# The same block products for key and gate tiles, with the last two products of a pair exchanged and its bank sums in another order

## The reference

```python
def mlstm_project(h, w_in, b_in):
    p = h @ w_in + b_in
    q, k, v, o, gates = jnp.split(p, [hk, 2 * hk, 2 * hk + hv, 2 * hk + 2 * hv], axis=-1)
    ...
```

## Time and profile before

| | us |
|---|---|
| median of 3 runs | 2078.43 |
| lowest and highest run | 2077.24, 2079.9 |
| profiled execution, from its first to its last instruction (span) | 2076.5 |
| TensorE busy in it | 2014.3 |
| VectorE, ScalarE, GpSimd busy in it | 1223.6, 819.1, 989.1 |

### The profile page before, as it was taken

How to read it: one execution, slowest core, us unless ns; L and a number is a source line. 1 busy time by engine, 2 the same in 40 slices (tenths; PEclk the granted TensorE clock), 3 DMA queues, 4 the chain that set the end, 5 groups by cost and what they waited for, 6 DMA issues and landing times.

```text
span 2076.5 us, 24039 instructions
## 1 busy us (share of the span) xinstructions
PE 2014.3 (97%) x9167; PEld 1663.5 (80%) x9167; DVE 1223.6 (59%) x1276; ACT 819.1 (39%) x1066; POOL 989.1 (48%) x560
## 2 busy tenths in 40 slices
PE   6999999999999999999999999988999999999999
PEld 5788888888788888878887888766788888878877
DVE  6889998877642475545502565589655555523125
ACT  5343355566452323221123464445344334412135
POOL 1376655555222222123311446648877877722244
PEclk7999999999999999999999999999999999999999
DMA  9641122122112323448855865341222222253123
GB/s 377 216 142 41 54 63 63 56 68 74 41 61 81 121 83 101 146 115 283 278 161 160 279 230 163 93 151 61 62 61 61 80 83 87 66 193 125 46 89 127
DMA packets 269263, 251.42 MB, mean 121 GB/s; under 512 B 8330, under 2 KB 230291, under 8 KB 269155
## 3 DMA queue, kind: packets, MB, share of 16 engines
q1 hardware_dynamic: 266067, 238.42, 36.3%
q10 hardware_dynamic: 3088, 11.54, 1.4%
HBM read 206.08 MB, written 43.84 MB: 120 GB/s over the span
## 4 chain that ended last, share of the span: by engine, by line
PE 51%; issue 14%; POOL 6%; DVE 1%; DMA 1%; ACT 0%; POOLq 0%; SPq 0%; DVEq 0%; ACTq 0%
PE PS L2227 16%; PE PS L1739 16%; PE PS L2005 5%; PE PS L2119 5%; POOL wl L851 3%; PE PS L2241 1%; PE PS L2063 1%; PE PS L2064 1%; PE PS L2072 1%; POOL SCR L1042 1%; PE PS L1928 1%; PE PS L2052 1%; PE PS L2153 1%; POOL wl L1029 1%; POOL XL L1025 0%
## 5 line engine op out<-in xcount | busy, mean ns | idle before, releaser
L851 POOL TENSOR_TENSOR wl<-raw,wh 128x1024 fp32r<-128x1024 f32 (+1 forms) x157 | 377.6, 2406 | 807.9 <-ACT wh L1098 589.7
L1739 PE MATMUL PS<-XH,wh 128*128 128x512 f32 x1424 | 442.4, 392 | 7.2 <-POOL wl L851 3.0
L1739 PE MATMUL PS<-XH,wl 128*128 128x512 f32 x1424 | 441.1, 391 | 0.0
L1739 PE MATMUL PS<-XL,wh 128*128 128x512 f32 x1424 | 440.6, 391 | 0.0
L1739 PEld LDWEIGHTS PS<-XH,wh 128*128 128x128 f32 x1424 | 264.9, 188 | 64.0 <-POOL wl L851 4.0
L1739 PEld LDWEIGHTS PS<-XL,wh 128*128 128x128 f32 x1424 | 265.7, 188 | 54.1
L1739 PEld LDWEIGHTS PS<-XH,wl 128*128 128x128 f32 x1424 | 265.4, 188 | 53.5
L1098 ACT ACTIVATE wh<-raw 128x1024 fp32r<-128x1024 f32 (+1 forms) x108 | 111.0, 1028 | 436.9 <-PE PS L1739 187.2
L2470 DVE SCALAR_TENSOR_TENSOR PS<-B,PJ,PS 128x1022 f32<-128x1022 f32 (+7 forms) x197 | 251.1, 1275 | 7.5
L1171 ACT ACTIVATE wh<-raw 128x1024 fp32r<-128x1024 f32 x48 | 50.8, 1058 | 248.2 <-PE PS L1739 228.7
L1029 POOL TENSOR_TENSOR wl<-SCR,wh 128x512 fp32r<-128x512 f32 x80 | 114.2, 1429 | 69.7 <-ACT wh L1567 69.1
(11 more groups left out here) (439 smaller groups left out, 3747.8 us busy)
## 6 DMA issues: line engine op xcount, KB each, us to landing
B<-in_ada_w SPq DMA_DIRECT2D x48, 512.0 KB, 5.4
raw<-in_ffn_up_w SPq DMA_DIRECT2D x48, 512.0 KB, 4.1
raw<-in_w_in SPq DMA_DIRECT2D x40, 512.0 KB, 4.5
raw<-in_m_in_w SPq DMA_DIRECT2D x37, 512.0 KB, 5.0
mod_tiles<-in_mod_w SPq DMA_DIRECT2D x16, 512.0 KB, 13.2
raw<-in_w_out SPq DMA_DIRECT2D x16, 512.0 KB, 5.0
qkvo_d<-B SPq DMA_DIRECT2D x16, 512.0 KB, 3.5
raw<-in_m_out_w SPq DMA_DIRECT2D x16, 512.0 KB, 4.2
```

The lines of the kernel that those rows point to most:

```text
L851: tt(wl[slot][:, 0:kc, :], raw[slot][:, 0:kc, :], wh[slot][:, 0:kc, :].bitcast(F32), ALU.subtract).then_inc(lo_done, 1)
L1739: last = mm(ps[:, c:c + step_n], W[:, k, :], Y[:, k, c:c + step_n], start=(seen == 0), stop=(seen == total - 1))
```

## The change

The four key tiles and the eight tiles of o are no longer projected one by one. They become six pairs (O_PAIRS; the first two, K_PAIRS, are keys) of seven block products each, all of them after the value passes. In a pair, the products come in the order O_ORDER, the last two exchanged against the up projection, and VectorE adds the banks in the order O_SUMS. For this:

- The tokens need sums and differences too. VectorE makes twelve tiles of 128x512 (token_sum, two or three operations each), ScalarE their high halves (token_high) and GpSimd their low halves (token_low), all during the value passes. A fourth set (t3_sum: twelve operations on GpSimd) replaces the second half of XH and XL in blocks 0 to 3 when the value passes are over; its low halves (t3_low) stand on VectorE's list between the first bank sums of pair 0.
- The reversing copies stand behind the first evacuation of values. SyncE waits for the ten row stores before it loads the ninth value unit, and ScalarE and VectorE wait for them too.
- Of the 32 late tiles four are multiplied during the value passes and 28 behind the 28 bank sums of pairs 0 to 3, one each. TensorE waits for all 32 before pair 4, transposes the gate rows there, and runs the 32 columns inside pair 4.
- Biases, sigmoid, scale and the store of a pair's tiles are ScalarE's (o_finish), the store issued from its own queue.
- Two value units are loaded ahead of the wait for the gate rows' chain (lf_sb).

```diff
--- before.py
+++ after.py
...
+        def o_bank(q):
+            b = (q + (2 if q >= 7 * (O_PAIRS - 2) else 0)) % 8
+            return part(PS[b // 2], b % 2)
+
+        O_ORDER = (0, 1, 2, 3, 4, 6, 5)
+        O_SUMS = (1, 4, 3, 6, 3, 2, 5)
+
+        def o_place(q):
+            s, n = divmod(q, 7)
+            return s, O_ORDER[n]
...
+            for u in range(4, V_UNITS):
+                proj_unit(V_FIRST + u)
+                if u in (6, 10, 14):
+                    v_store((u - 6) // 4)
+                if u == 7:
                     rows_store()
-                if t == O_UNIT + 1:
                     sp.wait_ge(*at("rows_out", 16 * 10))
+                if u == V_UNITS - 1:
+                    for n in range(4):
+                        late_load(n)
...
+            def pair_load(s):
+                for v in range(2):
+                    if s == 0:
+                        sp.wait_ge(lo_done, PAIR_UNIT + 1 + v)
+                    else:
+                        sp.wait_ge(*at("oq_lo", 7 * s - 5 + v))
+                        sp.wait_ge(*at("os_ok", 4 * s))
+                    if s < O_PAIRS:
+                        sp.dma_start(raw[(PAIR_UNIT + v) % 2][:], cols_of(m_in_w, 0, KD, o_column(s) + P * v)).then_inc(ev(f"oq_in{v}"), 16)
+                    else:
+                        half_unit(v)
...
+            pair_load(0)
+            v_store(3)
+            for s in range(O_PAIRS):
+                pair_load(s + 1)
+                if s == 1:
                     for n in range(3):
                         sp.wait_ge(*at(f"v_out{n}", 16 * len(range(n, NCH * 2, 3))))
                     sp.dma_start(ROWS, rows_d[0:NCOL, :]).then_inc(ev("gate_rows_in"), 16)
+                if s < O_PAIRS - 2:
+                    for n in range(4 + 7 * s, 4 + 7 * (s + 1)):
+                        late_load(n)
+                elif s == O_PAIRS - 2:
+                    sp.wait_ge(*at("late_summed", LATE * KD))
                     for d in range(2):
                         chunk_load(0, d, 0, False)
...
+            sp.wait_ge(*at("late_ps", 1))
+            chunk_load(1, 0, 1, False)
+            sp.wait_ge(*at("oq_used", 7 * (O_PAIRS - 1) + 4))
+            chunk_load(1, 1, 1, False)
...
+            def t3_sum(n):
+                k, i = divmod(n, 3)
+                if i == 0:
+                    tt(t3_t[k], XH[:, k + HK, HALF:SEQ].bitcast(F32), XH[:, k, HALF:SEQ].bitcast(F32), ALU.subtract).then_inc(ev("t3_sum"), 1)
+                elif i == 1:
+                    if k:
+                        pool.wait_ge(*at("t3_sum", n - 1))
+                    tt(US[:], XL[:, k + HK, HALF:SEQ].bitcast(F32), XL[:, k, HALF:SEQ].bitcast(F32), ALU.subtract).then_inc(ev("t3_sum"), 1)
+                else:
+                    pool.wait_ge(*at("t3_sum", n))
+                    tt(t3_t[k], t3_t[k], US[:], ALU.add).then_inc(ev("t3_sum"), 1)
+
...
+            T3_AT = {0: (0, 2), 1: (2, 4), 2: (4, 6), 3: (6, 8), 4: (8, 9), 14: (9, 12)}
+            LOW_AT = {7: (0, 2), 9: (2, 4), 10: (4, 6), 11: (6, 8), 12: (8, 10), 13: (10, 12)}
+            for u in range(1 - Q_TILES, V_UNITS):
+                low(GxG.U + V_FIRST + u, (GxG.U + V_FIRST + u) % 2)
+                if u == 0:
+                    pool.wait_ge(*at("xl_Gx", KD))
+                elif u == 14:
+                    pool.wait_ge(*at("rows_out", 16 * 10))
+                for n in range(*T3_AT.get(u, (0, 0))):
+                    t3_sum(n)
+                for m in range(*LOW_AT.get(u, (0, 0))):
+                    token_low(m)
+
...
+            for q in range(7 * O_PAIRS):
+                o_low(q)
+                s, i = divmod(q, 7)
+                if 1 <= q <= 4:
+                    o_weight_sum(0, q - 1)
+                elif 6 <= q <= 9:
+                    o_weight_sum(1, q - 6)
+                elif i in (5, 6) and 0 < s < O_PAIRS - 1:
+                    for n in range(2 * i - 10, 2 * i - 8):
+                        o_weight_sum(s + 1, n)
+            low(G5.U, G5.U % 2)
...
+            HIGH_AT = {7: (0, 2), 9: (2, 6), 10: (6, 9), 11: (9, 12)}
+            for u in range(1, V_UNITS):
+                high_at(GxG.U + V_FIRST + u, 0)
+                if u == 7:
+                    act.wait_ge(*at("rows_out", 16 * 10))
+                for m in range(*HIGH_AT.get(u, (0, 0))):
+                    token_high(m)
+
+            def o_high(q):
+                s, i = o_place(q)
+                if i < 3:
+                    act.wait_ge(*at(f"oq_in{i // 2}", 16 * (s + 1)))
+                else:
+                    act.wait_ge(*at("os_ok", 4 * s + i - 2))
+                if q < 4:
+                    act.wait_ge(unit_used, PAIR_UNIT + 1 + q // 2)
+                else:
+                    act.wait_ge(*at("oq_used", q - 3))
+                f(ring(wh, q), o_weights(i), ACT.Copy).then_inc(ev("oq_hi"), 1)
+
+            def o_copy(s):
+                act.wait_ge(*at("oq_used", 7 * s + 1))
+                if s:
+                    act.wait_ge(*at("osum_ok", SUMS * s))
+                f(US[:], o_bank(7 * s), ACT.Copy).then_inc(ev("opair_copy"), 1)
...
+            for q in range(4):
+                o_high(q)
+            for k in range(HK):
+                act.wait_ge(*at("t3_sum", 3 * k + 3))
+                f(XH[:, k, HALF:SEQ], t3_t[k], ACT.Copy).then_inc(ev("t3_hi"), 1)
+            for s in range(O_PAIRS):
+                o_high(7 * s + 4)
+                o_copy(s)
+                if s:
+                    o_finish(s - 1, 0)
+                o_high(7 * s + 5)
+                o_high(7 * s + 6)
+                if s < O_PAIRS - 1:
+                    for i in range(4):
+                        o_high(7 * (s + 1) + i)
+                    o_finish(s, 1)
...
+            o_finish(O_PAIRS - 1, 1)
+            o_finish(O_PAIRS - 1, 0)
...
+            def o_product(s, i):
+                q = 7 * s + O_ORDER.index(i)
+                (W_H, W_L), (X_H, X_L) = (ring(wh, q), ring(wl, q)), o_tokens(i)
+                bank = o_bank(q)
+                pe.wait_ge(*at("oq_lo", q + 1))
+                earlier = [p for p in range(q) if o_bank(p) == bank]
+                if not earlier:
+                    pe.wait_ge(*at("v_sb", q + 13))
+                else:
+                    before, j = o_place(earlier[-1])
+                    if j == 0:
+                        pe.wait_ge(*at("opair_copy", before + 1))
+                    else:
+                        pe.wait_ge(*at("osum_ok", SUMS * (before + 1) - O_SUMS[::-1].index(j)))
+                if q == 7 * (O_PAIRS - 1):
+                    pe.wait_ge(*at("late_used", 1))
+                if s == 0 and i == 2:
+                    pe.wait_ge(*at("tk_lo", 3 * HK))
+                elif s == 0 and i == 6:
+                    pe.wait_ge(*at("t3_lo", HK))
+                for k in range(HK):
+                    for n, (W, Y) in enumerate(((W_H, X_H), (W_L, X_H), (W_H, X_L))):
+                        ins = mm(bank, W[:, k, :], Y[:, k, :], start=(k == 0 and n == 0), stop=(k == HK - 1 and n == 2))
+                        c = 12 * (i - 1) + 3 * k + n
+                        if s == O_PAIRS - 2 and 0 <= c < LATE * KD:
+                            late_column(c)
+                ins.then_inc(ev("oq_used"), 1)
+
+            for s in range(O_PAIRS):
+                if s == O_PAIRS - 2:
+                    pe.wait_ge(*at("gate_rows_in", 16))
+                    pe.wait_ge(*at("opair_copy", s))
+                    pe.wait_ge(*at("late_summed", LATE * KD))
+                    for c in range(NCH):
+                        last = nc.tensor.transpose(COLS_BANK[:, NCOL * c:NCOL * (c + 1)], ROWS[:, P * c:P * (c + 1)], ident[0:NCOL, 0:NCOL])
+                    last.then_inc(ev("cols_ps"), 1)
+                for i in O_ORDER:
+                    o_product(s, i)
...
+            def token_sum(m):
+                i, k, full = block_sum(m)
+                if m >= 4:
+                    dve.wait_ge(*at("tk_lo", m - 3))
+                x12, x11, x22, x21 = ((XH[:, c, h:h + HALF].bitcast(F32), XL[:, c, h:h + HALF].bitcast(F32))
+                                      for c, h in ((k, HALF), (k, 0), (k + HK, HALF), (k + HK, 0)))
+                if i == 0:
+                    step.link(V.tensor_tensor(full, x12[0], x11[0], ALU.subtract))
+                    step.link(V.tensor_tensor(full, full, x12[1], ALU.add))
+                    V.tensor_tensor(full, full, x11[1], ALU.subtract).then_inc(ev("tk_sum"), 1)
+                else:
+                    x = x22 if i == 1 else x21
+                    dve.wait_ge(*at("tk_sum", m))
+                    step.link(V.tensor_tensor(full, x[0], holes[(m - 1) % 4], ALU.subtract))
+                    V.tensor_tensor(full, full, x[1], ALU.add).then_inc(ev("tk_sum"), 1)
+
+            def bank_sum_pair(s, n):
+                i = O_SUMS[n]
+                dve.wait_ge(*at("oq_used", 7 * s + max(O_ORDER.index(j) for j in O_SUMS[:n + 1]) + 1))
```

(36 more changed lines are left out.)

274 lines of the change are left out of this document (145 added, 129 removed).

## The result

The changed kernel takes 2116.21 us (median of 4 runs, 2113.47 to 2120.20) against 2077.84 (2077.22 to 2079.90, 4 runs) before: a ratio of 1.0181, 95% interval 1.0161 to 1.0200. It is slower by 38 us, on the forecast's side and inside its range; the forecast was 2110.

A forecast was written before the change was run, and what follows sets the result against it. TensorE, busy 97% of the span, bounds the kernel, so removed products gain and added waits lose. Steps 1 to 8 add 50.2 us, less 17.8 removed: +32 on 2078.4, forecast 2110 us, range 2080 to 2128.

The forecast's parts named there:

- Removed, 17.8: TensorE's projections: 72 fewer products save 16.3 us and a 1.44 us wait goes, 17.8 us in all.
- Step 1: Value passes: gate rows' chain on VectorE, in turns with GpSimd, delays the first value evacuation; TensorE waits 7 us.
- Step 2: Value passes: SyncE waits for the row stores before loading the ninth value unit; TensorE waits 6 us.
- Step 3: Value passes: second evacuation stands behind token sums taking turns with GpSimd, 3.5 us; ScalarE's units wait likewise, 2 us.
- Step 4: Pair 0: its sixth product waits for low token tiles behind late sums on VectorE, 7 us.
- Step 5: Before pair 4: TensorE waits for all 32 late products, 7 us without turns, 14.7 with all, 11 taken.
- Step 6: Pairs 1 to 3: VectorE's lag, 21.8 us excluding GpSimd in a 19.04 us period, delays first-bank copies, 6 us.
- Step 7: End: the first weighed key waits for the last bank sum and a copy, 1.7 us.
- Step 8: Clock: TensorE is granted a lower clock behind some of the waits, 6 us lost.
- The rival by GpSimd and VectorE together: Pairs bound by both engines' excluding work, period 21.8 us or more in pairs 0 to 3: about +45, 2123; chance 0.17.
- one SBUF input does not contend: VectorE beside GpSimd: only instructions with two SBUF inputs take turns; a bank sum with one PSUM input keeps 0.69 us.

The follow-up runs named there:

- a1: Changed kernel with nine of twelve GpSimd token differences moved from behind value units 0 to 4 to behind units 5 to 9: 2118.64 us, ratio 1.0187.
- c1: Changed kernel with the nine GpSimd token differences behind value units 0 to 4 left out: 2115.03 us, ratio 1.0165.
- a3: Changed kernel where pairs 1 and 3 write their first tile into another buffer, so first bank sums wait for no store: 2105.14 us, ratio 1.0134.
- a4: Changed kernel without the 28 late tiles of pairs 0 to 3, neither loaded nor multiplied: 2082.39 us, ratio 1.0022.
- b2: Changed kernel with TensorE's wait for the late products moved to before pair 4's fourth product, columns inside its last three: 2107.01 us, ratio 1.0126.
- a2: Changed kernel with all four low token tiles behind pair 0's first bank sum, ahead of the first late sum: 2114.56 us, ratio 1.0164.
- b3: Changed kernel with products and bank sums in the up projection's order, finishing a pair's first tile with the fourth sum: 2109.78 us, ratio 1.0135.
- d1: c3 with fewer late loads ahead of a pair's weights and the last three token differences spread over units 12, 13, 15: 2085.41 us, ratio 1.0030.
- b1: Changed kernel with value passes reordered: first two evacuations earlier, row stores behind the tenth unit's load, token halves later: 2117.36 us, ratio 1.0181.
- c2: Changed kernel with b1's value passes (value stores earlier, last token halves later), b3's order, a2's low tiles, b2's columns, late sums earlier: 2116.72 us, ratio 1.0168.
- c3: As c2, but with the changed kernel's own order of products and bank sums and a3's second buffer: 2095.27 us, ratio 1.0073.

## Why the prediction was right

The direction and its reason were right: not the removed matmuls decide, but what the other engines must do beside the rest. By its steps:

- **Removed, 17.8.** Right: 72 matmuls fewer, and the 1.44 us wait is gone.
- **Step 1, chain.** Predicted 7, measured 7.4. Its cause, turns with the token differences, is shown: a1 and c1 take the differences away, the chain then starts 4.2 us sooner and takes 4.6 less, and the wait is gone. The weight lows keep the remaining turns (21.9 us for the 15.7 free of them). That the number fits so well is luck: the step had the chain start at its old place and take 29 to 31 us; it took 26.5 and started 4.2 us late, by turns of the small operations ahead of it, and the two errors cancel.
- **Step 2, rows and ninth unit.** Predicted 6 (its own times, 946.9 less 941.6, give 5.3), measured 0.5. Three durations were too long: the ten stores took 6.5 us of SyncE (925.71 to 932.2, its next load at 934.98) for 8.1, the unit landed 3.8 us after its issue for 4.9, and the evacuations took 4.2 for 5.2. As the lateness is one line, part of what was not waited for here was waited for at step 3.
- **Step 3, second evacuation.** 3.5 and ScalarE's 2 predicted, 5.7 and 0.7 measured; in the executions of a3, a4 and b2 no 5.7, and 1.6 for the 0.7. Steps 1 to 3 together: 18.5 predicted, 14.4 measured.
- **Step 4, sixth product.** Predicted 7, measured 8.2, for the reason given; a2 shows that it is not additive: 3.6 of the 8.2 us come back behind it, since the pairs are late anyway.
- **Step 5, before pair 4.** Predicted 11, measured 12.6, and this too is luck. Without the loop of the stores it is 7.5, 4.8 of it before pair 4 (a3): what the step has without turns (7). The turns that it added are there, but cost 0.3 us each (1.56 to 1.6 us a late sum for 1.3) and not up to 1.28. The loop, which it does not have, made up for them.
- **Step 6, pairs 1 to 3.** Predicted 6 from GpSimd's and VectorE's shared 21.8 us, measured 8.7. The step names the wrong bound: the pace of 25 to 26 us a pair is that of last sum, copy, finish, store, landing, first sum. The prediction had the wait at proj_out in its diff and never priced it. a3 and b3, which open the loop in different ways, show it: the sums' waits for the stores go, and TensorE's waits in pairs 1 to 3 are 5.5 and 3.5 us.
- **Step 7, end.** 1.7 predicted; the wait there is 2.4 us for the 0.9 that it was. It stands behind the stage.
- **Step 8, clock.** Predicted 6, measured 10.7 in the stage, for nothing before.

The sum of what was added to the stage, without step 7: 48.5 predicted, 39.4 + 17.8 = 57.2 measured. Steps 1 to 3 were 4.1 too high together, steps 4 to 6 5.5 too low and step 8 4.7 too low; the other 2.6 are in pieces too small to be listed. So the forecast lies 6 us from the result partly because a bound that it did not have, the stores, stood in for turns that it priced too high.

The rival by GpSimd and VectorE together (2123) names a true mechanism that was not the bound of the changed kernel: its pairs came 25 to 26 us apart by the loop of the stores, not 21.8. Whether it is the floor beneath, no run settles. a4 can't, since it takes VectorE's half of the excluding work away too. The copies of the first bank come 23.9 to 25.6 us apart in a3 and 22.6, 22.8, 24.1 and 19.8 in d1, with all operations done; b3 has one of 21.05. The Trainium skill (SBUF — State Buffer, Who interferes with whom) has the engine that issues first keep the shared port pair for its whole instruction while the other blocks. The traces agree in the stretched operations of both engines, and a1 shows the consequence: GpSimd's work that was moved along a busy VectorE took most of the wait with it. The prediction's "one SBUF input does not contend" held for the bank sums (0.69 us throughout), not for the copies (4.93 us for four of 4x256).

Left open: why b1 and c1, whose stages are 6.7 and 8.8 us shorter in the profiled execution, are 0 and 3 us faster in the runs (known to 5 us either way; a1's 2.7 us lie inside that). The executions of a1 and c1 had lost 7 us before the stage began (885.17 and 885.27 for 878.22), in code that is unchanged.

## What to carry to other kernels

When a tile is finished in a buffer that the next round writes first, write down the whole loop, from the last sum over the store's landing to the first sum, and set it against the round; the order of the sums decides how much of it is serial. The 512 KB stores of a4, without the late loads, landed in 4.5 us (median), those of the changed kernel, beside seven such loads a pair, in 9.3, so the loop must be priced with the loads around it. Waits along one line of dependences do not add up: what is taken off the first place lets TensorE come sooner to the next (b1, c1), so the whole line has to be followed to its last place. And look at what stands behind a wait: one of 2.7 us was followed in c2 by 27 us at 1.2 GHz, 13 us more than c3 needed for the same products.

## What the runs showed that was not expected

- Turns are also taken by copies on 4 partitions: four copies of 4x256, 2.04 us alone, take 4.93 beside GpSimd, and one of 9 elements on 36 partitions took 2.15 us in a1 where the changed kernel has 0.95. How small an operation is does not save it from waiting for the other engine's whole one.
- The same instructions of the value passes gave a wait of 5.7 us or none. In the changed kernel's execution, with the wait, the last two of the reversing copies took 3.13 us, in a3's, without it, 1.00.
- In d1 the clock fell to 0.66 of 2.4 GHz in the window behind a wait of 1.78 us (ended 1034.96), and stayed at 1.00 behind the one of 2.40 us at 1041.61:

```profile
1035.00:1040.00 5.00, 4.21 (x12) 2.85 (x12) 4.93 (x5) 0.63 (x1) 4.95 (x3) 0.66 0.68 238
...
1040.00:1045.00 5.00, 3.39 (x15) 2.79 (x16) 1.82 (x3) 1.40 (x2) 5.00 (x4) 1.00 0.32 81
```
